# Stage seams of a nine-stage decoder kernel: single-producer waits, norms by token halves, early weight splits, hinted branches, output in four pieces

## The reference

```
h = rms_norm(x, g);  x = x + even_mixer(h)      # RWKV-7 heads beside causal pooling   (even)
h = rms_norm(x, g);  x = x + hier_moe(h)        # 4 groups x 8 experts, top 2          (moe0)
h = rms_norm(x, g);  x = x + odd_mixer(h)       # differential attention beside S5     (odd)
h = rms_norm(x, g);  x = x + hier_moe(h)        #                                      (moe1)
for l in 0, 1:
    x = x + hybrid_mixer(rmsnorm(x, w))         # retention beside SSD                 (hyb0, hyb1)
    x = x + swiglu(rmsnorm(x, w))               # 1024 -> 2 x 2816 -> 1024             (ffn0, ffn1)
return rmsnorm(x, w)                            #                                      (fin)

rms_norm(x, g) = x * rsqrt(mean(x * x, axis=-1) + 1e-6) * g
```

## Time and profile before

| | |
|---|---|
| median of 3 runs | 2895.92 us (2891.4 to 2906.26) |
| profiled execution | 2896.71 us, of which the span is 2894.8 us |
| busy PE / weight loads | 2355.3 us (81%) / 1789.2 us (62%) |
| busy DVE / ACT | 1266.0 us (44%) / 908.5 us (31%) |
| mean granted TensorE clock | 0.911 |
| DMA | 663.24 MB, mean 229 GB/s |

### The profile page before, as it was taken

The page is one execution under the profiler, slowest core; times in us unless marked ns, Lnnn a source line. Parts: engine busy times, 40 slices in busy tenths (PEclk is TensorE's granted clock), DMA queues, the critical chain, the costliest instruction groups (busy, mean ns, idle before and its releaser), DMA issues.

```text
span 2894.8 us, 37242 instructions
## 1 busy us (share of the span) xinstructions
PE 2355.3 (81%) x16380; PEld 1789.2 (62%) x16380; DVE 1266.0 (44%) x1879; ACT 908.5 (31%) x1249; POOL 2.5 (0%) x8
## 2 busy tenths in 40 slices
PE   8876666765687666666599899898989989988898
PEld 7675212211464321212199899788979989978896
DVE  3574222221373210111256468645555646864554
ACT  3132000000123100000144467634444446763443
POOL 0000000000000000000000000000000000000000
PEclk9988988888898788888799999999999999999999
DMA  5202899999604799999844353434444435343452
GB/s 228 90 1 88 358 427 428 428 427 428 279 15 176 293 427 429 427 427 428 340 149 172 120 190 122 155 124 175 181 160 152 169 120 189 117 162 120 153 193 95
DMA packets 48094, 663.24 MB, mean 229 GB/s; under 512 B 5296, under 2 KB 5552, under 8 KB 7344
## 3 DMA queue, kind: packets, MB, share of 16 engines
q1 hardware_dynamic: 47344, 657.39, 56.7%
q0 software_dynamic: 576, 3.32, 0.3%
HBM read 659.64 MB, written 1.05 MB: 228 GB/s over the span
## 4 chain that ended last, share of the span: by engine, by line
PE 40%; DVE 5%; ACT 5%; issue 1%; DVEq 0%; ACTq 0%
PE ps L2128 8%; PE ps L2129 8%; PE ps L2130 8%; DVE r L2118 2%; PE ps L2363 2%; PE ps L2364 2%; PE ps L2365 2%; ACT r L2107 2%; PE ps L2921 1%; PE ps L2920 1%; PE ps L2919 1%; PE ps L2170 1%; PE ps L2168 1%; PE ps L2169 1%; PE ps L2292 1%
## 5 line engine op out<-in xcount | busy, mean ns | idle before, releaser
L2118 DVE TENSOR_TENSOR r<-ring,r 128x1024 fp32r<-128x1024 f32 (+1 forms) x360 | 502.0, 1403 | 442.9 <-ACT r L2107 442.6
L2128 PE MATMUL ps<-r 128*128 128x256 f32 x2112 | 611.6, 290 | 17.8 <-DVE r L2195 13.3
L2129 PE MATMUL ps<-r 128*128 128x256 f32 x2112 | 601.7, 285 | 0.0
L2130 PE MATMUL ps<-r 128*128 128x256 f32 x2112 | 601.3, 285 | 0.0
L2107 ACT ACTIVATE r<-ring 128x1024 fp32r<-128x1024 f32 (+1 forms) x360 | 425.3, 1197 | 357.9 <-PE ps L2130 184.2
L640 PE MATMUL ps<-ring,arena 128*32 128x512 f32 x2048 | 309.8, 738 | 205.8 <-DMA ring<-w_dram 204.0
L2128 PEld LDWEIGHTS ps<-r 128*128 128x128 f32 x2112 | 409.3, 194 | 25.7 <-DVE r L2195 14.8
L2129 PEld LDWEIGHTS ps<-r 128*128 128x128 f32 x2112 | 409.6, 194 | 0.3
L2130 PEld LDWEIGHTS ps<-r 128*128 128x128 f32 x2112 | 409.3, 194 | 0.0
L640 PEld LDWEIGHTS ps<-ring,arena 128*32 128x32 f32 x2048 | 63.2, 122 | 442.8 <-DMA ring<-w_dram 272.2
L663 PE MATMUL ps<-ring,arena 128*32 128x512 f32 x1024 | 149.3, 715 | 94.0 <-DMA ring<-w_dram 94.0
(11 more groups left out here) (415 smaller groups left out, 3348.1 us busy)
## 6 DMA issues: line engine op xcount, KB each, us to landing
ring<-w_dram SPq DMA_DIRECT2D x305, 2048.0 KB, 24.9
ring<-w_dram SPq DMA_DIRECT2D x12, 1024.0 KB, 4.8
cst<-w_dram POOLq DMA_DIRECT2D x2, 973.0 KB, 6.9
x<-x_dram SPq DMA_DIRECT2D x1, 1024.0 KB, 6.4
ring<-w_dram SPq DMA_DIRECT2D x2, 512.0 KB, 13.4
out_dram<-x SPq DMA_DIRECT2D x1, 1024.0 KB, 4.0
ring<-w_dram SPq DMA_DIRECT2D x1, 768.0 KB, 15.1
cst<-w_dram POOLq DMA_DIRECT2D x1, 704.0 KB, 8.2
```

The costliest lines, as they stand in the source:

```text
L2118: v.tensor_tensor(lo, w, hi.bitcast(F32), SUB).then_inc(*S.up(f"lo {s}", *(["free " + name] if last else [])))
L2128: pe.matmul(out, hi[:, k, :], K.HH[:, k, :], start=k == 0, stop=False)
L2129: pe.matmul(out, hi[:, k, :], K.HL[:, k, :], start=False, stop=False)
L2130: r = pe.matmul(out, lo[:, k, :], K.HH[:, k, :], start=False, stop=k == 7)
```

## The change

What it does:

- `begin` is gone from all stages but the first. A norm waits for the quarters of X that it reads (`half_ready`), each named by its last addition.
- All squares are taken by ACT, a quarter at a time (`squares_act`): the first quarter's sum is scaled with eps by an `Identity`, the second's goes through `Sqrt` with that as its bias. A tiny `Sqrt` at the head (`root_ready_act`) waits for nothing. Each half has a reciprocal and a scaling of its own, DVE scaling features 0 to 511 and ACT 512 to 1023.
- DVE takes half 0's reciprocal and scaling ahead of the last addition of the stage before (`next_half_dve`), except behind a moe stage. PE transposes all of half 0, then all of half 1.
- PE's first product waits for features pair by pair (`wait_features`), not for all.
- In even and odd the last products go half 0 first. In moe stages the loops over n and t change places.
- In hyb and ffn two tiles are split at the end of the stage before. At moe1 to hyb0, ACT splits tiles 0 and 1 ahead of the norm, behind the landing of the first chunk. Tile 2 is split after HH.
- The overflow flag is loaded at the head of the last q; a branch with a prefetch hint, marked there, takes the place of the `If`, and the wait for all stands inside the body that is not entered. Kept gates are written once, early.
- The fin stage works by halves and quarters, and X is stored in four DMAs.
- The norm's buffers move within the arena, and one parameter column is added.

```diff
+def squares_act(K, a, st, t, n):
+    S, b = K.sig[st, "act"], norm_bufs(K, st)
+    half_ready(K, a, st, t, n)
+    cs, ss = slice(n * 512, (n + 1) * 512), [b.ss[:, i:i + 1] for i in (2 * t, 2 * t + 1, 4 + t)]
+    a.activation(b.xn[:, t, cs], K.X[:, t, cs], ACT.Square, accum_out=ss[n]).then_inc(*S.up())
+    a.wait_ge(*S.now())
+    if n == 0:
+        a.activation(ss[2], ss[0], ACT.Identity, bias=K.par("eps6"), scale=1.0 / 1024).then_inc(*S.up())
+    else:
+        a.activation(ss[2], ss[1], ACT.Sqrt, bias=ss[2], scale=1.0 / 1024).then_inc(*S.up(f"{st} root{t}"))
+def norm_act(K, a, st):
+    root_ready_act(K, a, st)
+    squares_act(K, a, st, 0, 0)
+    squares_act(K, a, st, 0, 1)
+    squares_act(K, a, st, 1, 0)
+    if after_moe(K, st):
+        squares_act(K, a, st, 1, 1)
+        scale_act(K, a, st, 0)
+    else:
+        scale_act(K, a, st, 0)
+        squares_act(K, a, st, 1, 1)
+    scale_act(K, a, st, 1)
+def norm_half_dve(K, v, st, t):
+    rstd_dve(K, v, st, t)
+    v.wait_ge(*S.now())
+    v.tensor_scalar(b.xn[:, t, 0:512], K.X[:, t, 0:512], b.ss[:, 6 + t:7 + t], None, MUL).then_inc(*S.up(f"{st} xv{t}"))
+def next_half_dve(K, v, st):
+    if K.stage_after(st):
+        norm_half_dve(K, v, K.stage_after(st), 0)
+def wait_features(K, pe, st, k):
+    if k % 2 == 0:
+        pe.wait_ge(*K.after(f"{st} nT{k} read"))
...
+def over_flag(K, e, st, l):
+    e.wait_ge(*K.after(st + " flag"))
+    return e.value_load(K.FLAG[0:1, l:l + 1], min_val=0, max_val=1 << 20), e.mark_branch_hint_location()
+@contextmanager
+def over_path(K, e, st, name, flag, hint):
+    more, done = f"{st}_{name}_more", f"{st}_{name}_done"
+    e.br_lt(flag, 1, on_true=done, on_false=more).branch_hint(hint)
+    with e.bass.body(more, valid_engines=bass.OrderedEngineSet([e.engine])):
+        for sem, n in K.ends(st):
+            e.wait_ge(sem, n)
+        yield
+    e.bass.switch_bb(done)
...
 def norm_HL_act(K, a, st, first):
-    scale_act(K, a, st)
-    cut_act(K, a, S, K.first_tile[first] + AHEAD)
+    if after_moe(K, st):
+        if K.stage_before(st):
+            a.wait_ge(*K.after(f"{K.stage_before(st)} y{NE // 4 - 1}"))
+        cut_act(K, a, S, K.first_tile[first] + 1)
+    norm_act(K, a, st)
...
 def norm_HL_dve(K, v, st, first):
-    scale_dve(K, v, st)
-    cut_dve(K, v, S, K.first_tile[first] + AHEAD)
+    norm_dve(K, v, st)
+    cut_dve(K, v, S, K.first_tile[first])
...
+    cut_dve(K, v, S, K.first_tile[first] + 1)
...
     for i in range(2):
         j = K.first_tile[f"{st}_wo{i}"]
         cut_dve(K, v, S, j + 2)
-        cut_dve(K, v, S, j + 4)
+        cut_dve(K, v, S, j + 5)
         for t in range(2):
             xs = K.X[:, t, i * 512:(i + 1) * 512]
+            if i and t:
+                next_half_dve(K, v, st)
...
+    out = K.out_d.rearrange("(t p) d -> p t d", p=128)
+    for t in range(2):
+        for n in range(2):
+            cs = slice(n * 512, (n + 1) * 512)
+            sp.wait_ge(*K.after(f"{K.stages[-1]} X{t}{n}"))
+            sp.dma_start(out[:, t, cs], K.X[:, t, cs]).then_inc(K.s_out, 16)
```

More of the change, by code:

```diff
@@ L261, in restart, with keep @@
         self.cut = {"a": 0, "v": 0}
+    def keep(self, name, of):
+        b = of.of[name]
+        self.banks.of[name] = b
+        for banks in (self.banks, self.low, self.high):
+            if b in banks.order:
+                banks.held[b] = name
     def after(self, name):
@@ new lines, in next_half_dve, with norm_dve @@
+def next_half_dve(K, v, st):
+    if K.stage_after(st):
+        norm_half_dve(K, v, K.stage_after(st), 0)
+def norm_dve(K, v, st):
+    if after_moe(K, st):
+        norm_half_dve(K, v, st, 0)
+    norm_half_dve(K, v, st, 1)
+def norm_pe(K, pe, st):
+    S, b, ident = K.sig[st, "pe"], norm_bufs(K, st), K.par("ident", 0, 128)
+    of, p = K.high if K.stage_before(st) == "odd" else K.banks, {}
+    for t in range(2):
+        for k in range(0, 8, 2):
+            name = f"{st} nT{k}"
+            if t == 0:
+                p[k] = bank(K, pe, name, of)
+                K.keep(name, of)
+            if k == 0:
+                pe.wait_ge(*K.after(f"{st} xv{t}"))
+            elif k == 4:
+                pe.wait_ge(*K.after(f"{st} xa{t}"))
+            for kk in (k, k + 1):
@@ L685, in moe_act @@
         u = q % 2
+        if q == NE // 4 - 1:
+            flag, hint = over_flag(K, a, st, l)
         a.wait_ge(*K.after(f"{st} g{q}"))
@@ L811, in moe_dve @@
         u = q % 2
+        if q == NE // 4 - 1:
+            flag, hint = over_flag(K, v, st, l)
         if q < NE // 4 - 1:
@@ L894, in over_act, with over_dve @@
         over_end(K, a, l)
-def over_dve(K, v, st, l):
+def over_dve(K, v, st, l, flag, hint):
     b, (done, act, pe, dma), G = over_bufs(K), K.over[l], kept_gates(K, l)
-    with v.If(over_begin(K, v, st, l) > 0):
+    with over_path(K, v, st, "dve", flag, hint):
         for e in range(NE):
@@ L1550, in added @@
             xs = K.X[:, t, i * 512:(i + 1) * 512]
-            v.wait_ge(*K.after(f"even {name}{i}{t}"))
-            tt(xs, K.banks[f"even {name}{i}{t}"], xs, ADD, f"even {name}{i}{t} read")
+            v.wait_ge(*K.after(f"even pout{i}{t}"))
+            tt(xs, K.banks[f"even pout{i}{t}"], xs, ADD, f"even pout{i}{t} read")
             yield
             yield
-    staggered([(EVERY * hp, chunks(hp)) for hp in range(4)] + [(3, added("pout"))])
-    for _ in added("out"):
-        pass
+    staggered([(EVERY * hp, chunks(hp)) for hp in range(4)] + [(3, pooled())])
+    out_proj_dve(K, v, S, st, K.banks)
 def odd_bufs(K):
@@ L1792, in odd_pe @@
     out(3, True)
-    for n in range(4):
+    for n in (0, 2, 1, 3):
         out(n, False)
@@ L2281, in hyb_pe @@
     ones, ident = K.par("ones", 0, 128), K.par("ident", 0, 128)
-    begin(K, pe, st)
     norm_pe(K, pe, st)
-    pe.wait_ge(*K.after(f"{st} nT6 read"))
     def sums(w, name, n, ready):
@@ L2903, in ffn_pe @@
         for j, part in ((0, "g"), (2, "u")):
[L2904 removed]
+            for _ in proj_pe(K, pe, S, c + j, f"{st} {part}{i}", first=None if i or j else st):
                 pass
```

234 lines of the change are left out of this document (111 added, 123 removed).

## The result

| | kernel before | changed kernel |
|---|---|---|
| median of the runs (us) | 2898.6 (2891.4 to 2906.3, 4 runs) | 2861.2 (2860.7 to 2867.5, 4 runs) |
| profiled execution (us), span | 2896.7, 2894.8 | 2861.4, 2859.6 |
| mean granted TensorE clock | 0.911 | 0.914 |

The ratio is 0.9876, 95% interval 0.9845 to 0.9906: 37 us faster. Forecast were 49. The time lies in the whole range of the forecast, 2834 to 2866, but 8 us outside the 2839 to 2853 that the forecast gave to its own case. The sum behind it was 13 us too large, and most of what follows is about these.

A forecast was written before the change was run, and what follows sets the result against it. Mixture stages bound by DMA, hyb and ffn by TensorE, even and odd by short dependent steps, with holes between; gains 45.7 + 3 for the clock take 2896.7 to 2848.0, median 2847. Own case 2839 to 2853, whole range 2834 to 2866.

The forecast's parts named there:

- The five short seams: Even to moe0 and odd to moe1, 5.1 us gain each; into ffn0 and ffn1 5.5 each; into hyb1 5.0.
- The end: After the last add to X, halved norm work and quarter stores gain 2.35 + 1.8, say 4.0 us.
- moe0 to odd: From moe0 into odd: projection at 761.05 instead of 770.91, gain 9.9 us if neither DVE nor PE waits for instructions.
- the jump still stalls: Rival at the branch out of moe0: hint fails, 5.2 us lost on DVE or 3.4 on PE alone; chance 0.2.
- moe1 to hyb0: Into hyb0: PE can begin at about 1441.7 instead of 1446.38, gain 4.7 us, or 3.4 with table load behind splits.
- The start: Kernel's first product at 13.9 instead of 14.8 us, since it waits for single features; gain 0.9 (0 to 1.4).
- Insides of the stages: Within every stage: no inside changes length by more than 2 us, else the forecast is wrong.
- The clock: TensorE spends less time at the lower clock behind shorter holes: 3 us gain taken, bounds 0 and 11.
- The split of the second tile ahead: At hyb and ffn ends: one split fewer before the features, last add later; no separate gain given.
- pieces don't overlap: Rival: each seam but moe0 to odd gives back half its gain, 18 us, and the clock's 3: 2868; chance 0.06.
- does nothing: Rival: another wait holds the engines until the old time at most seams, within 14 us of before; chance 0.02.
- slower: Rival: the hint costs PE instruction fetches of 5.8 us each in both mixtures, 2911 us and more; chance 0.02.

The follow-up runs named there:

- the one of the gains together: Changed kernel with VectorE's early branch, no second input wait at the start, norm ahead of the first copies into hyb0, and 21648 arena columns: 2837.5 us, ratio 0.9789.

## Why the forecast was near, and where its steps failed

*The five short seams* (even to moe0, odd to moe1, and the three late ones) were forecast at 26.2 us together and gave 29.0 in holes, 26.8 with the later last adds taken off. The mechanism is shown by the run with the waits undone. What I took too high is ScalarE's price per quarter, 1.0 us: it is 0.94, as the starts at 8.99 and 9.93 of the start's squares show. I had also let the last add be 0.8 and 1.46 us late; it was 0.5 and 1.2. The hole at hyb0 to ffn0 was to be 4.6 and is 4.57. The end was forecast at 4.0 and gave 4.8, 4.1 with its later add taken off: a store of 256 KB took 2.0 us, where I had 2.2, and the formula of the Trainium skill, "DMA: Bandwidth & Descriptors", had 2.6. The page gives it for transfers that GpSimd issues; SP issued these, and the measured time decides.

*moe0 to odd* is the rival "the jump still stalls", and it came nearly as priced, 4.5 us lost where the rival had 5.2, on VectorE alone. My step took it as given that the hint removes the stall, and gave the rival 0.2. On TensorE it does (0.4 us instead of 6.1), so the step was half right, and the rival's 3.4 us for TensorE alone were not lost. Runs without hint, without bodies and with bodies apart show that on VectorE the hint has no effect at this place and that the distance is the cause. The earlier trace rows gave reason for more than 0.2: they showed the jump's price and nothing that a hint had ever removed.

*moe1 to hyb0* was forecast at 4.7, or 3.4 if the table load comes behind the copies. It does (1421.52), and the gain was 2.6. The load took 8.4 us instead of 7.7. That the copies ahead of the norm are the wrong order was in my working as a cost; that turning it round frees the whole seam once VectorE's jump is gone too (7.38) I hadn't seen.

*The start* was forecast at a gain of 0.9 and lost 1.3. Two terms failed: the table load moved behind the landing of x, where it costs its full 1.28 us, and I had not looked at what the second wait ahead of it does; and single features gave nothing, since ScalarE with four half squares is as late as VectorE and ScalarE with one row each were.

*Insides of the stages* were to stay within 2 us, and that sign of being wrong came true: bodies together 2613.3 us before and 2619.8 after. The cause wasn't in any step. It is the arena's size: the pace of the products that read behind it accounts for some 6 of the 6.5 us. With 21648 columns the bodies together are 2606.7, less than before the change, and all late seams run at 2.4 GHz in that trace. 45.7 less the 4.5 of the jump, the 2.2 of the start and the 2.1 of moe1 to hyb0, plus 0.7 from the short seams and the end, are 37.6. The stretches from first to 121st product gave 4.1 more, and 6.5 went back inside the stages: 35.2.

*The clock* was to give 3. The stretches behind the first products of ffn0, hyb1 and ffn1 are 1.8 us shorter than before, 1.4 of it at hyb1, where the clock now stays at 2.4 GHz; the rest of the 4.1 is spread over the other five and can't be put down to the clock. What I had too high is its price. I took one less the clock, times the stretch: 3.3 us for 7 us at 0.53. In the traces it costs 1.9 a seam.

That the time with the arena's size back, 2847.8, is the number I forecast is chance: the terms of the jump, the start and moe1 to hyb0 are missing, and the hybrid bodies, which I had left as they were, are 7.3 us shorter than before.

*The split of the second tile ahead*, which I had costed as part of the late seams' gain, is worth nothing by itself.

*The rivals "pieces don't overlap" and "does nothing"* are refuted by the table, *"slower"* too: without hints the time is the same, so that nothing of what the hint might cost TensorE shows in it. The 0.03 us between dependent steps, which I read from the earlier trace rows, are the shortest such gap; in the same rows 0.10 lie between the last add and the square and 0.15 between the scaling and the first transpose.

## What to carry over

- A wait for all of a stage is paid in every engine's chain. Waits for single pieces gave 23 of 37 us here; ask for each first instruction of a stage which one producer it needs.
- A branch over a long body that is nearly never entered costs the jump over it each time. Write the body out of line, or branch where the engine is idle anyway. A hint took 6 us off TensorE's branch and nothing off VectorE's: look at the branch of every engine before calling it useful or useless.
- When an edit changes the size of a buffer, compare the addresses of all that is allocated behind it, and compare the rate of the same products in both traces before looking at waits. Eight columns took a quarter of this change's gain away.

## What the runs showed of the hardware

- VectorE needed 5.5 to 6.5 us from a branch to its next instruction when the jump passed some hundreds of its own instructions, with a prefetch hint and without, and 0.6 us when the body was short or elsewhere. ScalarE with a body of 32 operations needed 0.6 us either way.
- TensorE's branch over its long body took 6.1 to 6.9 us without a hint and 0.35 to 0.40 us with one 56 us ahead.
- A table load is done ahead of a single wait of its activation (0.73 us in, x lands at 7.5) but stays behind a separate second one (7.59).
- The feed forward stages' down products, with a 512 column operand, came every 229.0, 233.4 or 226.7 ns, steady over whole stages, when all that lay behind the arena moved by 32 or 64 bytes. The hybrid stages' output products came every 118.9 ns in all nine kernels with the one address and every 114.1 to 116.4 in three with the other.
- Behind a hole of 4.3 to 4.6 us, the granted clock over 7 us was 0.53 in some traces and 1.00 in others, and two kernels with the same arena fell on different sides (the one with 21648 columns and the one of the gains together); it costs 1.9 us a seam when it falls.
